# Prompt attention of a hybrid decoder step: products four steps behind their scores, seven turned groups, the compressed product moved

## What is computed

```python
s_c = einsum(q, kc); p_c = masked_softmax(s_c, m_c); o_c = einsum(p_c, vc)     # 63 compressed blocks
s_s = einsum(q, ks); p_s = masked_softmax(s_s, m_s); o_s = einsum(p_s, vs)     # selected blocks
s_w = einsum(q, kw); p_w = masked_softmax(s_w, m_w); o_w = einsum(p_w, vw)     # window of 512
o = g[..., 0:1] * o_c + g[..., 1:2] * o_s + g[..., 2:3] * o_w
```

## Time and profile before

| what | us |
| --- | --- |
| median of 3 runs | 3793.62 |
| lowest and highest run | 3791.02, 3802.79 |
| span of the profiled execution | 3797.9 |
| TensorE busy in it | 3627.8 |
| prompt attention in it, about 2252 to 2783 | 531 |

### The profile page before, as it was taken

One profiled execution on the slowest core, in us unless ns is written; L12 is line 12 of the kernel. 1 busy time (PEld: TensorE's weight loads), 2 busy tenths in 40 slices (PEclk: granted clock), 3 DMA queues, 4 the chain that ended last, 5 costly groups with the idle time before them and its releaser, 6 DMA issues. The chain is left out here.

```text
span 3797.9 us, 53113 instructions
## 1 busy us (share of the span) xinstructions
PE 3627.8 (96%) x19730; PEld 2803.0 (74%) x19730; DVE 2196.1 (58%) x3358; ACT 968.6 (26%) x2167; POOL 1634.2 (43%) x1573
## 2 busy tenths in 40 slices
PE   8999999998899999999999889989989999999999
PEld 5777777776668888878868666766667788887887
DVE  4666556675476555566642135555555655556666
ACT  3334443334211111100001015555541111111002
POOL 0121112211246999943421114443423399996432
PEclk9999999998899999999999999999999999999999
DMA  4111111111331221262333310000033212214522
GB/s 155 33 46 34 35 46 28 41 45 40 121 122 48 72 73 57 80 202 86 82 113 75 80 32 15 1 1 2 1 115 100 81 52 74 68 57 136 158 77 86
DMA packets 307889, 262.75 MB, mean 69 GB/s; under 512 B 30650, under 2 KB 283699, under 8 KB 305651
## 3 DMA queue, kind: packets, MB, share of 16 engines
q1 hardware_dynamic: 301988, 253.14, 21.9%
q0 software_dynamic: 2048, 5.25, 0.5%
q10 hardware_dynamic: 3650, 1.64, 0.2%
HBM read 212.97 MB, written 51.08 MB: 70 GB/s over the span
## 5 line engine op out<-in xcount | busy, mean ns | idle before, releaser
L1779 PE MATMUL ps<-xn,work 128*128 128x363 f32 (+1 forms) x1536 | 545.2, 473 | 1.3 <-ACT work L2070 1.1
L393 PE MATMUL ps<-work 128*128 128x272 f32 x1612 | 384.7, 394 | 16.9 <-PEq L1601 7.3
L393 PEld LDWEIGHTS ps<-work 128*128 128x128 f32 x1612 | 306.6, 191 | 84.6 <-issue 21.5
L960 PE MATMUL ps<-work 128*128 128x272 f32 x1360 | 367.2, 392 | 0.0
L960 PE MATMUL ps<-xT,work 128*128 128x272 f32 x1280 | 340.6, 394 | 9.7 <-POOL work L1263 9.7
L1779 PEld LDWEIGHTS ps<-xn,work 128*128 128x128 f32 x1536 | 258.6, 190 | 95.0 <-issue 8.5
L3474 POOL TENSOR_SCALAR work<-work 128x640 f32<-128x640 f32 (+7 forms) x256 | 198.4, 784 | 288.0 <-DVE work L3384 287.9
L960 PE MATMUL ps<-xn,work 128*128 128x272 f32 x1280 | 319.8, 392 | 0.0
L960 PEld LDWEIGHTS ps<-work 128*128 128x128 f32 x1360 | 258.4, 190 | 53.3
L692 POOL TENSOR_TENSOR xT<-xT,work 128x272 f32<-128x272 f32 x96 | 195.4, 2048 | 227.1 <-DVE work L543 144.8
L960 PEld LDWEIGHTS ps<-xT,work 128*128 128x128 f32 x1280 | 241.7, 190 | 66.2 <-POOL work L1263 17.4
(11 more groups left out here) (488 smaller groups left out, 6745.5 us busy)
## 6 DMA issues: line engine op xcount, KB each, us to landing
work<-in_ffn_w_in_dram SPq DMA_DIRECT2D x160, 256.0 KB, 3.3
xn<-in_ffn_w_out_dram SPq DMA_DIRECT2D x46, 704.0 KB, 4.7
work<-in_gdn_w_in_dram SPq DMA_DIRECT2D x32, 512.0 KB, 4.1
work<-in_ffn_w_out_dram SPq DMA_DIRECT2D x18, 704.0 KB, 4.5
work<-in_gdn_w_out_dram SPq DMA_DIRECT2D x44, 256.0 KB, 3.6
ffn_parked_hidden_late<-work SPq DMA_DIRECT2D x20, 544.0 KB, 2.9
work<-ffn_parked_hidden_late SPq DMA_DIRECT2D x2, 5440.0 KB, 23.2
ffn_parked_residual<-xT SPq DMA_DIRECT2D x2, 4352.0 KB, 13.9
```

The source lines that it names most:

```text
L393: mm = pe.matmul(acc(n, a), w[:, k, :], t[:, k, :], start=(first and k == 0), stop=(k == hk - 1), skip_group_check=True)
L960: ins = pe.matmul(acc(a, n), w[:, k, :], t[:, k, :], start=(first and k == 0), stop=(k == 1), skip_group_check=True)
L1779: mm = pe.matmul(unit_acc(u, m), w[j % 2][:, k, :], c.xn[:, k, o:o + cnt], start=(k == 0), stop=(k == KD - 1))
```

## The change

On PE the products run four steps behind the scores instead of three (`LAG`), so that they follow their turns by two steps instead of one. The ring has seven places instead of four; the three new ones lie in a free part of `c.xTf`, which the names show as xT. The compressed product of query block i leaves `turns_of` of ("w", i) and goes to the end of the loop body in which the products of ("s", i) are made; the wait for the kept compressed groups goes with it. ACT's `output` is four steps behind too. Maxima, exponentials, scaling, turning and keeping stay where they are. The loops of PE and ACT have one more round.

```diff
--- before.py
+++ after.py
@@ -3154,8 +3154,9 @@
     NK = len(steps)
     step_of_c = {t: k for k, (t, kind, i) in enumerate(steps) if kind == "c"}
     dead = a.kvT[:, 0:2, :].rearrange("p k t -> p (k t)")
-    RING = 4
-    pts = [dead[:, n * 512:(n + 1) * 512] for n in range(RING)]
+    RING, LAG = 7, 4
+    spare = c.xTf[:, 6 * D:6 * D + (RING - 4) * 512]
+    pts = [dead[:, n * 512:(n + 1) * 512] for n in range(4)] + [spare[:, n * 512:(n + 1) * 512] for n in range(RING - 4)]
     low = [a.rows[:, n, 2 * P:3 * P].bitcast(BF16) for n in range(4)]
     ident_low, causal_low, far_low = low[0][:, 0:P], low[0][:, P:2 * P], low[1][:, 0:P]
     cmp_low = [low[2 + x][:, 0:4 * NCMP] for x in range(2)]
@@ -3302,9 +3303,6 @@
 
                     t, kind, i = steps[k]
                     pe.wait_ge(scaled, k + 1)
-                    if kind == "w" and i == 0:
-                        for x in range(2):
-                            group_kept(step_of_c[t], x)
                     pe.nop(nofuse=True)
                     for x, gr in enumerate(groups(k)):
                         if order[k, x] >= 3:
@@ -3313,8 +3311,16 @@
                             src = pc[:, n, :] if kind == "c" else buf(k, g)[:, n * P:(n + 1) * P]
                             mm = pe.transpose(turn_bank(k, x)[:, m * P:(m + 1) * P], src, const(c, "ident"))
                         mm.then_inc(tr, 1)
-                    if kind == "w":
-                        pe.matmul(bank(c, 7)[:, 0:P], a.vcp, pcts[t % 2][:, i, :], start=False, stop=False, skip_group_check=True)
+
+                def compressed_products_of(k):
+                    t, kind, i = steps[k]
+                    if kind != "s":
+                        return
+                    if i == 0:
+                        for x in range(2):
+                            group_kept(step_of_c[t], x)
+                        pe.nop(nofuse=True)
+                    pe.matmul(bank(c, 7)[:, 0:P], a.vcp, pcts[t % 2][:, i, :], start=False, stop=False, skip_group_check=True)
 
                 def products_of(k):
                     t, kind, i = steps[k]
@@ -3335,13 +3341,15 @@
                         mm.then_inc(multiplied, 1)
 
                 pe.wait_ge(low_ready, 1)
-                for k in range(NK + 3):
+                for k in range(NK + LAG):
                     if k < NK:
                         scores(k)
-                    if 3 <= k:
-                        products_of(k - 3)
+                    if LAG <= k:
+                        products_of(k - LAG)
                     if 2 <= k < NK + 2:
                         turns_of(k - 2)
+                    if LAG <= k:
+                        compressed_products_of(k - LAG)
 
             @block.vector
             def _(dve):
@@ -3448,11 +3456,11 @@
                         act.wait_ge(multiplied, ring_of[k, len(groups(k)) - 1] + 1)
                         act.activation(c.xn[:, t, i * P:(i + 1) * P], bank(c, 7)[:, 0:P], ACT.Copy).then_inc(od, 1)
 
-                for k in range(NK + 3):
+                for k in range(NK + LAG):
                     if k < NK:
                         exps(k)
-                    if 3 <= k:
-                        output(k - 3)
+                    if LAG <= k:
+                        output(k - LAG)
                     if 2 <= k < NK + 2:
                         keep(k - 2)
```

## The result

| what | before | after |
| --- | --- | --- |
| median, 9 runs each, us | 3793.62 | 3809.68 |
| all runs, us | 3791.0 to 3802.8 | 3806.6 to 3815.2 |
| ratio of after to before, 95% interval | | 1.0042, 1.0031 to 1.0054 |
| span of the profiled execution, us | 3797.9 | 3807.3 |
| PE's first turn of c to its last product, us | 522.8 | 532.4 |

The change makes the kernel slower by 16 us between these medians (0.42%), where 7.7 us and no measurable change were forecast and 3808 was the top of the range. The stretch that it touches grew by 9.6 us in the two profiled executions.

A forecast was written before the change was run, and what follows sets the result against it. PE was taken as the bound, busy 484.9 of 532 us in prompt attention. The terms 0.1 + 5.6 + 0.9 + 1.1 gave +7.7 us, median 3793.6 to 3801.3, range 3793 to 3808.

The forecast's parts named there:

- The c step, gain 0: At the c step, PE's 1.67 us wait for ACT's keep becomes waits for ACT's output copy and POOL; gain 0.
- the 9.85 us chain: From the scores of c to its turns, through PE, DVE and POOL: 9.85 us, every link untouched by the change.
- Behind the c step, long rounds: In the long rounds, ("w", 6) and ("w", 7) hold fewer product records and no compressed product; gain 0.6 us per head.
- The backlog: In the short steps, 24 more product records and one compressed product make the next c step 1.54 us later.
- The sum of the order: First c step 0.1, six intervals of +0.94 5.6, last head 0.9, end 1.1: together +7.7 us; chance 0.57.
- The clock: Rival: PE's waits at c steps lower its clock, 1.15 us a fall, 3808.2; 0.2 together with waits for ACT's output.
- The range: Whole time 3793 to 3808 us, leaving out the vanished gap (0.09) and the clock's far end (about 0.08).
- The rule on recurring gaps: Rival at PE's wait for ACT's keep: the longer ring wins all 11.7 us, net -10.4, 3783.2; chance 0.09.
- The rule on the clock: A wait in every tile makes TensorE's clock fall in every tile; the trace was said to agree in one of seven.

The follow-up runs named there:

- e5: Before with the ring of seven and products, compressed products and outputs four steps behind only in the four rounds from the c step on; 65.72 us a head, ratio 1.0014.
- e11: After with identity matmuls that nobody reads placed in PE's two waits at each c step; 66.57 us a head, prompt attention 529.0 us, ratio 1.0037.
- e1: The kernel before run again without an edit; 65.72 us a head, prompt attention 521.6 us, ratio 1.0005.
- e2: The changed kernel run again without an edit; 66.57 us a head, prompt attention 533.2 us, ratio 1.0036.
- e9: Before with the two changed orders of e8 and the turns of c with their keeps one round later; 64.27 us a head, ratio 0.9972.
- e3: Before with only the ring enlarged to seven places, products still three steps behind; 65.70 us a head, ratio 1.0006.
- e12: The changed kernel, products four steps behind, with the changed orders and later turns of c of e9; 65.47 us a head, ratio 1.0018.
- e8: Before with, at each c step, DVE's coefficients ahead of its maxima and ACT's keep ahead of its exponentials; 65.65 us a head, ratio 1.0016.
- e4: Before with only the compressed product moved to the end of the round with its s step's products; 65.95 us a head, ratio 1.0020.

## Why the prediction was wrong, point by point

- **The c step, gain 0.** Right: e5 shows it, and the 9.85 us chain was untouched. The output copy and POOL took the keep's place, 2.45 us of waiting where 2.5 was said.
- **Behind the c step, long rounds.** Right in sum: 0.60 us back per head, as said. The waits for exponentials grew to 25.0 us and not to 27. Falls of the clock are not the reason, since e11, which has none, shows 25.1; where the missing 2 us went stays open.
- **The backlog.** The term was 1.54 us per head and is 1.45; +0.94 per interval was +0.85.
- **The sum of the order.** +7.7 was said, 7.4 is what e11 and e1 show, and the parts agree too. From PE's first turn of c to the scores of c that stand in head 1, e11 takes 1.06 us longer than e1 (0.1 + 0.94 was said), over the five intervals behind it 4.3 (4.7 was said), and from there to the end 2.1 (2.0 was said).
- **The clock.** This is the step that failed. More falls of the clock were put as a rival at 0.2 (with waits for ACT's output), deciding from three more falls, and left out of the sum. In the traces there are three and four more than in the profiled before. The price was missed as well: 0.83 to 0.89 us in after and not the 1.15 of before. In prompt attention the falls are worth 3.4 and 4.2 us, from 529.0 without a fall to 532.4 and 533.2; with the 7.4 of the order that is 10.8 and 11.6 against 521.6.
- **The range.** The order and the falls in prompt attention alone, 10.8 us, would give 3804.4 from the median shown, inside the range; the median is 3809.7. A later comparison gave a ratio of 1.0036 (12 us between the medians), so the gap is not that of one comparison alone.
- **The rest goes with the clock too.** For most runs the mean granted clock is on record. In 81 runs of before, in three later comparisons, it lies between 0.983 and 0.991, and a straight line through them falls by 2.3 us of time for each 0.001 of clock, with 2.5 us of scatter (one standard deviation) left around it. The runs of the changed kernel average 0.9830 and 0.9835, before's 0.9872. Held against that line at their own clock, the nine first runs are 7.0 us slower than before, e2's eight 5.6, e11's ten 8.6, and e9's ten are 10.3 faster (its trace: 511.4 - 521.6 = -10.2). So the order of the work shows in the whole times at about its forecast size, and some 9 of the 16 us go with a lower clock in the whole program, where the sum had nothing. This is an estimate: for the nine runs of before in the first comparison no clock is on record. The fall shown above takes 3.40 x (1 - 0.52) = 1.6 us of full clock, or 0.0004 of the program's, so the four or five in prompt attention make up about half of the 0.004 that the changed kernel lacks. What lowers the clock outside prompt attention stays open. Before without an edit came to 0.9859 (e1, twelve runs) beside 0.9874 (31 runs of the same comparison), so a part need not belong to the change.
- **The rule on recurring gaps** (the Trainium skill, "Perfetto Trace Analysis", Optimization Strategy). A gap that recurs can mean too few buffers, it says; the ring alone (e3) and the distance at the c step alone (e5) won nothing, so here the measurement decides against that reading.
- **The rule on the clock** (the Trainium skill, "TensorE: Matmul & The Clock Gate", HAM oscillation), that a wait in every tile can bring a fall in every tile, deserved more weight than it got: the traces of the changed kernel agree at four or five of seven, and in no trace here does the clock fall at every one. The page's own case has longer waits, for DMA. The length of the wait does not order the falls here: two of seven behind 2.23 us (e5), two behind 1.97 (e12), three in e8, whose longest wait is 1.33.

## What to carry to other kernels

A wait that recurs is worth its size only if no longer chain spans it: measure from the chain's first work to its last on the timeline before moving anything, and take the end of the chain out of the way first (here 10 us, for one round's delay of turns that nobody needed yet, together with two changed orders on DVE and ACT). A longer distance between producer and consumer carries its backlog from phases where the engine waits into phases where it does not, so price it as the difference of the open sets between the two. And where an engine's clock can fall after a wait, count the falls in more than one trace before they are left out of a sum, and compare whole times only beside the granted clock of the runs.

## What the runs showed of the hardware

TensorE's clock fell at none or one of seven c steps in the four traces with PE's wait at 1.67 us in the orders of before (before, e1, e3, e4), and at four or five of seven with it at 1.79 (after, e2). The length of the interval changed too (65.72 and 66.57 us), and kernels with longer waits had fewer falls (2.23 us: two; 1.97 us: two), so the length of the wait alone does not decide it. Identity products in the waits took all falls away at the same interval, in one trace; the same products behind the long wait took none away. In the traces of after and e2 the same four c steps fell (e2 had the first as well).

Most of the scatter of whole times goes with the granted clock: 2.3 us for each 0.001 in 81 runs of before, which leaves a standard deviation of 2.5 us around the line, where the times themselves lie between 3785.6 and 3803.9. Head periods without a fall came back to 0.02 us from trace to trace.
